# A hybrid decoder layer on one core: the first chunk's order around its constants, attention, second norm and first expert head

## The reference

```python
hn = modulate(rmsnorm(x, g_norm1), sh1, sc1)
xr, gr, q, k, v, gate_r, gate_a = split(hn @ w_in)
xc = causal_conv(xr);  hseq = rglru(xc)            # gates r, i; linear scan over time
y_r = (hseq * gelu(gr)) @ w_rnn_out
y_a = attention(rope(q), rope(k), v, window 128, sinks) @ w_attn_out   # 16 heads, 4 key heads
merged = sigmoid(gate_r) * y_r + sigmoid(gate_a) * y_a
x1 = x + gt1 * (merged @ w_out)
h2 = modulate(rmsnorm(x1, g_norm2), sh2, sc2)
# expert mixer: 8 heads, two sets of 128 keys per head, top 16 of each, top 16 of their sums
s = (h2 @ w_pq) . sub_keys;  e, g = top16 of pairs, softmax
out[t] = sum over the 128 chosen experts of g * gelu(h2[t] . u_tab[e]) * v_tab[e]
y = rmsnorm(x1 + gt2 * out, g_final)
```

## Time and profile before

| | us |
|---|---|
| median of 3 runs | 2088.82 |
| the three runs | 2089.44, 2076.90, 2088.82 |
| profiled execution | 2075.17 |
| its span in the profile | 2073.4 |
| busy in the span: PE / DVE / POOL / ACT | 1382.4 / 1238.5 / 1131.1 / 514.2 |
| gathers of `u_tab` and `v_tab` | 520 + 520, 545.33 MB of 701.78 MB |

### The profile page before, as it was taken

One profiled execution on the slowest core, in us unless ns is written; L12 is line 12 of the kernel. 1 busy time (PEld: TensorE's weight loads), 2 busy tenths in 40 slices (PEclk: granted clock), 3 DMA queues, 4 the chain that ended last, 5 costly groups with the idle time before them and its releaser, 6 DMA issues.

```text
span 2073.4 us, 22570 instructions
## 1 busy us (share of the span) xinstructions
PE 1382.4 (67%) x7058; PEld 882.5 (43%) x7058; DVE 1238.5 (60%) x3120; ACT 514.2 (25%) x1466; POOL 1131.1 (55%) x1046
## 2 busy tenths in 40 slices
PE   5998999877877677988877876433444444543444
PEld 5877888766654444666555643111111110111111
DVE  3255211376888788766658656656667656655640
ACT  2436200222345244112213322112111112211110
POOL 0000000046664466757756767777777777777774
PEclk9999999988998898979888987555555666656556
DMA  9745345499999799999999999999999999999997
GB/s 349 263 155 201 118 139 172 139 343 400 369 407 344 272 342 341 408 393 376 408 407 403 374 409 388 391 369 376 377 385 366 397 386 386 373 385 379 374 396 281
DMA packets 202294, 701.78 MB, mean 338 GB/s; under 512 B 22552, under 2 KB 32096, under 8 KB 201888
## 3 DMA queue, kind: packets, MB, share of 16 engines
q0 software_dynamic: 149760, 545.33, 68.2%
q1 hardware_dynamic: 52416, 155.02, 20.7%
HBM read 691.26 MB, written 11.06 MB: 339 GB/s over the span
## 4 chain that ended last, share of the span: by engine, by line
PE 26%; DVE 19%; DMA 18%; issue 17%; POOL 17%; ACT 3%; SPq 1%; POOLq 0%; DVEq 0%; ACTq 0%
POOL arena L1894 17%; PE acc L738 15%; DMA arena<-in_v_tab,pku 9%; DVE arena L1741 6%; DMA arena<-in_u_tab,pku 5%; PE y L1030 5%; DMA arena<-key_rows 3%; PE acc L777 2%; DVE pku L1762 1%; DMA arena<-w_mod 1%; DVE pk L1761 1%; PE acc L751 1%; DVE arena L1468 1%; DVE pku L1774 1%; DVE arena L1514 1%
## 5 line engine op out<-in xcount | busy, mean ns | idle before, releaser
L1894 POOL DMA_INDIRECT arena<-in_u_tab,pku x520 | 566.4, 1089 | 599.8 <-DVE pku L1800 336.5
L1741 DVE CUSTOM_DVE_ANT_0 arena<-arena 128x1024 f32<-128x1024 f32 x520 | 625.8, 1223 | 388.1 <-DMA arena<-in_u_tab,pku 379.1
L1894 POOL DMA_INDIRECT arena<-in_v_tab,pku x520 | 561.7, 1080 | 241.9 <-issue 145.4
L1030 PE MATMUL y<-arena 128*32 128x512 f32 x2080 | 417.0, 919 | 411.2 <-DMA arena<-in_v_tab,pku 410.5
L738 PE MATMUL acc<-arena 128*128 128x256 f32 (+1 forms) x2816 | 658.9, 394 | 33.5 <-DVE arena L1421 13.1
L738 PEld LDWEIGHTS acc<-arena 128*128 128x128 f32 x2816 | 545.6, 196 | 159.9 <-issue 64.4
L1030 PEld LDWEIGHTS y<-arena 128*32 128x32 f32 x2080 | 81.8, 144 | 645.2 <-issue 625.2
L1013 PE MATMUL turned<-arena 128*128 128x256 f32 x128 | 60.0, 561 | 135.9 <-DVE arena L1817 133.1
L1013 PEld LDWEIGHTS turned<-arena 128*128 128x128 f32 x128 | 26.7, 252 | 202.6 <-DVE arena L1817 195.3
L1301 ACT ACTIVATE pk<-pk 128x1 f32<-128x1 f32 x520 | 103.6, 281 | 2.1
L1298 ACT ACTIVATE pk<-pk 128x8 f32<-128x8 f32 x65 | 13.5, 208 | 301.6 <-DVE pk L1741 278.3
(11 more groups left out here) (210 smaller groups left out, 1354.4 us busy)
## 6 DMA issues: line engine op xcount, KB each, us to landing
arena<-w_mod SPq DMA_DIRECT2D x48, 512.0 KB, 5.8
arena<-w_pq SPq DMA_DIRECT2D x32, 512.0 KB, 6.7
arena<-w_xr SPq DMA_DIRECT2D x20, 512.0 KB, 9.3
arena<-w_qk SPq DMA_DIRECT2D x20, 512.0 KB, 6.9
arena<-w_gr SPq DMA_DIRECT2D x20, 512.0 KB, 6.7
arena<-w_rnn SPq DMA_DIRECT2D x16, 640.0 KB, 4.0
arena<-in_u_tab,pku POOLq DMA_INDIRECT x520, 7.7
arena<-in_v_tab,pku POOLq DMA_INDIRECT x520, 6.8
```

Of the source, the lines that this page charges most:

```text
L1030: mm = pe.matmul(y[rows, h, :], spread[g % NTURN][:, 32 * j:32 * j + 32], rows_v[j][:, h * 512:(h + 1) * 512], start=first and (g != SAMPL ...
L1741: dve.tensor_tensor_reduce(u_row[j], u_row[j], h_of[o], 1.0, 0.0, ALU.mult, ALU.add, dots[g % 2][:, j:j + 1]).then_inc(s_urd, 1)
L1894: pool.indirect_dma_start(out=row, out_offset=None, in_=table, in_offset=bass.IndirectOffsetOnAxis(ap=idx, axis=0), **more).then_inc(signa ...
```

## The change

It moves work in the order of all engines, and adds little:

- **Constants.** The identity and ones stay where they were. The attention mask, the smaller constants and the convolution state are loaded after `mod` piece 15 and no longer ahead of pieces 4 to 15; cos and sin after them too. They get a semaphore of their own, for which `turned_rows` waits.
- **Rotations.** The second batch of five scans is cut into 2, 2 and 1, with the rotations of query blocks 2 and 3 between.
- **Gate blocks.** `gr` 0 goes in front of the first scores and `gr` 1 behind them, in both chunks, and each step has one `gr`.
- **Second norm, chunk 0.** The sum of squares goes into the bank `turned`, one matmul behind each `out` block and the last by itself; ACT loads the root's table before the `out` blocks. The k-th matmul of `pq` 0 waits for the k-th row block of `h2T` alone.
- **First scores.** A product `first` behind `pq` 1 gives the scores of head 0; `PEER_FROM` is behind it, so `pq` 2 and on belong to the second stretch. Places for pieces are dealt accordingly.
- **Later heads.** `load_stage` is issued two quarters earlier (but for heads 1 and 16); head 1 is ranked two quarters later.
- **End.** DVE scales the last tile's sums straight from the bank `y`; ACT copies nothing, and loads the root's table ahead.

```diff
+GR_EARLY = 2
+GR_AT = ((2,), (3,), (4,), (5,), (6,), (7,), (8,), (9,))
-GR_AT = ((0,), (1,), (2, 3), (4,), (5,), (6, 7), (8,), (9,))
...
         mods(ch, "scores")
+        block(ch, "gr", 0)
         product(ch, "s", 0, (), 0.9)
         product(ch, "s", 1, (), 0.9)
+        block(ch, "gr", 1)
...
                 block(ch, "pq", c)
+                if ch == 0 and c == 1:
+                    product(0, "first", 0, (("keys", 0),), 0.5)
-PEER_FROM = NO[0, "keys", 0] + 1
+PEER_FROM = NO[0, "first", 0] + 1
-RANK_FROM = [PARTS * g - 2 * PARTS for g in FIRST_GROUP]
+RANK_FROM = [PARTS * g - 2 * PARTS + 2 * int(h == 1) for h, g in enumerate(FIRST_GROUP)]
+STAGE_AT = [f + 1 if h in (1, CT * PH) else f - 1 for h, f in enumerate(RANK_FROM)]
...
-                sp.dma_start(const[:, b:b + 4 * P], X["const"][:, a:a + 4 * P]).then_inc(s_const, 16)
+                sp.dma_start(const[:, b:b + 2 * P], X["const"][:, a:a + 2 * P]).then_inc(s_const, 16)
+                load_until((0, "mod", 15))
+                a, b = CONST_COLS["mask"][0], LOCAL_COLS["mask"][0]
+                sp.dma_start(const[:, b:b + 2 * P], X["const"][:, a:a + 2 * P]).then_inc(s_const2, 16)
                 a, b, w = CONST_COLS["iota"][0], LOCAL_COLS["iota"][0], TOPK + NKV + 3 * P
-                sp.dma_start(const[:, b:b + w], X["const"][:, a:a + w]).then_inc(s_const, 16)
+                sp.dma_start(const[:, b:b + w], X["const"][:, a:a + w]).then_inc(s_const2, 16)
                 sp.dma_start(states[:, RC * 3:RC * 27], X["conv_state"]).then_inc(s_conv0, 16)
-                load_until((0, "mod", 7))
...
-                if k - 1 in RANK_FROM[1:]:
-                    load_stage(RANK_FROM.index(k - 1, 1))
+                if k in STAGE_AT[1:]:
+                    load_stage(STAGE_AT.index(k, 1))
...
+                    if name == "pq" and c == 0:
+                        pe.wait_ge(s_h, 2 * DC * ch + DC + k + 1)
                     mm = pe.matmul(a[:, 0:n], w[:, k, :], rhs[:, k, 0:n], start=(k == 0), stop=(k == ks - 1))
...
+            def sum_early(k):
+                pe.wait_ge(s_sq, DC + k + 1)
+                return pe.matmul(turned[:, 0:CP], ones, squares2[:, k, 0:CP], start=(k == 0), stop=(k == DC - 1), skip_group_check=True)
...
+            def first_scores():
+                wk = await_piece(pe, (0, "keys", 0))[:, 0:4 * P].rearrange("p (c k) -> p c k", c=4)
+                yield NO[0, "first", 0]
+                a = take(0, "first", 0)
+                for c in range(2):
+                    await_read(pe, 0, "pq", c)
+                    mm = pe.matmul(a[:, c * P:(c + 1) * P], pq[0][:, c, 0:P], wk[:, c, :], start=True, stop=True)
+                mm.then_inc(s_ready, 1)
...
                     project(ch, "out", c, mg)
+                    if ch == 0 and c:
+                        sum_early(c - 1)
...
+                if ch == 0:
+                    yield NO[ch, "out", 0]
+                    act.activation(fstat[:, 3:4], eps, ACT.Sqrt)
...
-                scans(ch, 1)
+                scans(ch, 1, (5, 6))
+                yield NO[ch, "turn", QK_THEN[0]]
+                rotate(ch, QK_THEN[0])
+                scans(ch, 1, (7, 8))
+                yield NO[ch, "turn", QK_THEN[1]]
+                rotate(ch, QK_THEN[1])
+                scans(ch, 1, (9,))
+                scanned(ch, 1)
...
+                if o == TILES:
+                    act.activation(fstat[:, 3:4], eps, ACT.Sqrt)
+                    return
...
+                else:
+                    dve.wait_ge(s_store, 16 * tile)
+                    dve.wait_ge(s_vrd, 2 * (LAST_GROUP[o] + 1))
+                    link(dve.tensor_tensor(dst.rearrange("p (h n) -> p h n", h=2), y[:, :, :], gain.rearrange("p (h n) -> p h n", h=2), ALU.mult))
```

More of the change, by code:

```diff
@@ L214, in _slots @@
         late = int(FIRST[p] >= PEER_FROM)
+        if p == (0, "keys", 0):
+            place[1] = place[0] % (OWN + EXTRA) + 1
         s = place[late] % (OWN if late else OWN + EXTRA)
@@ L916, in chunk @@
                 yield from modulations(ch, "scores")
+                yield NO[ch, "gr", 0]
+                project(ch, "gr", 0, hT)
                 yield NO[ch, "s", 0]
                 yield from att_scores(ch, 0)
+                yield NO[ch, "gr", 1]
+                project(ch, "gr", 1, hT)
                 for i in range(STEPS):
@@ L954, in chunk @@
                     project(ch, "out", c, mg)
+                    if ch == 0 and c:
+                        sum_early(c - 1)
                 yield NO[ch, "norm", 1]
-                pe.wait_ge(s_sq, ch * 2 * DC + 2 * DC)
-                square_sum(ch, 1, squares2)
+                if ch == 0:
+                    take(0, "norm", 1)
+                    sum_early(DC - 1).then_inc(s_ready, 1)
+                else:
+                    pe.wait_ge(s_sq, ch * 2 * DC + 2 * DC)
+                    square_sum(ch, 1, squares2)
                 yield from modulations(ch, "norm")
@@ L966, in chunk @@
                         project(ch, "pq", c, h2T)
+                        if ch == 0 and c == 1:
+                            yield from first_scores()
                     yield NO[ch, "keys", (CT + ch) * pair]
@@ L1010, in turn @@
                     pe.wait_ge(s_mask, 1)
+                    await_read(pe, 0, "norm", 1)
                 else:
@@ L1076, in root @@
                 a = take(ch, "norm", which)
+                if ch == 0 and which:
+                    a = turned
                 release(act.activation((rstd, rstd2)[which][:, 0:n], a[:, 0:n], ACT.Sqrt, bias=eps, scale=1.0 / D), ch, "norm", which)
@@ L1238, in chunk @@
                         release(act.copy(pq[c // PH][:, c % PH, 0:n], a[:, 0:n]), ch, "pq", c)
+                        if ch == 0 and c == 1:
+                            yield NO[0, "first", 0]
+                            a = take(0, "first", 0)
+                            release(act.copy(stage[0], a[:, 0:2 * NKEYS]), 0, "first", 0)
                     for t in range(CT + ch):
@@ L1241, in chunk @@
                         yield NO[ch, "keys", m]
-                        if ch == 0 and m == 0:
-                            a = take(ch, "keys", 0)
-                            act.copy(stage[0], a[:, 0:2 * NKEYS]).then_inc(s_first, 1)
                         spill_rows(ch, "keys", m, rows_of(t))
@@ L1459, in variances, with scans @@
                     link(dve.tensor_tensor(gate_i[:, i, 0:n], gate_i[:, i, 0:n], xc[:, j, 0:n], ALU.mult))
-            def scans(ch, b):
+            def scans(ch, b, js):
                 n = TOK[ch]
-                for j in range(HALF5 * b, HALF5 * b + HALF5):
+                for j in js:
                     i = j % HALF5
@@ L1633, in chunk @@
                 yield NO[ch, "qk", 9]
-                scans(ch, 0)
+                scans(ch, 0, range(HALF5))
+                scanned(ch, 0)
                 for c in QK_FIRST[:-1]:
@@ L1648, in chunk @@
                     dve.sem_inc(s_state, 1)
-                for c in QK_THEN[:-1]:
+                for c in QK_THEN[2:-1]:
                     yield NO[ch, "turn", c]
@@ L1664, in chunk @@
                         att_normalise(ch, i + 1)
+                    if i == 0:
+                        for c in range(GR_EARLY):
+                            gate_rows(ch, c)
                     for c in GR_AT[i]:
@@ L1753, in best_keys @@
                 if head == 0:
-                    dve.wait_ge(s_first, 1)
+                    await_read(dve, 0, "first", 0)
                 else:
@@ L1836, in add_residual @@
                 dst, x, gain = (ysum, xin, gt2p) if tile < TILES else (hcur[1], xin_s, gt2s)
-                dve.wait_ge(s_yfree, o + 1)
-                link(dve.tensor_tensor(dst[0:rows, :], dst[0:rows, :], gain[0:rows, :], ALU.mult))
+                if o < TILES:
+                    dve.wait_ge(s_yfree, o + 1)
+                    link(dve.tensor_tensor(dst[0:rows, :], dst[0:rows, :], gain[0:rows, :], ALU.mult))
+                else:
+                    dve.wait_ge(s_store, 16 * tile)
+                    dve.wait_ge(s_vrd, 2 * (LAST_GROUP[o] + 1))
+                    link(dve.tensor_tensor(dst.rearrange("p (h n) -> p h n", h=2), y[:, :, :], gain.rearrange("p (h n) -> p h n", h=2), ALU.mult))
                 if tile < TILES:
```

14 lines of the change are left out of this document (9 added, 5 removed).

## The result

| | before | after |
|---|---|---|
| median of six runs, us | 2080.16 | 2057.47 |
| lowest and highest | 2075.58, 2089.44 | 2053.24, 2066.78 |
| profiled execution, its span | 2075.17, 2073.4 | 2057.22, 2055.0 |

The ratio is 0.9889, with an interval of 0.9851 to 0.9927: 1.1% faster, 15 to 31 us. The forecast of 2062.5 and its range of 2045 to 2080 hold the median; the profiled execution gained 18.0 us where the sum said 26.3. By medians the gain is thus 22.7 us here and 26.9 there. The two traces, on which the account by stretches rests, show less of it.

A forecast was written before the change was run, and what follows sets the result against it. PE bounds the stretch before the first gather, DMA transfers the rest. Front 20.0, chunk 1's first scores 4 and end 2.3 sum to 26.3 us off 2088.82: 2062.5 us, range 2045 to 2080.

The forecast's parts named there:

- Transfers bound the rest: From the first gather on: DMA engines are full, so an earlier first ranking, by 20.0 us, comes off the end.
- Constants: Before `mod` 3: 0.72 MB of constants and states no longer load ahead of its pieces, 1.8 us.
- norm and `pq` 0: Chunk 0's second norm and first query block: one sum hidden (0.5 us), per-row wait removes 2.20; together 2.7 us.
- end: After the last sums: ACT's copy (1.01 us) falls away and the root's table load (1.28) moves earlier, 2.3 us.
- Gate blocks: Chunk 0 attention: `gr` 1 fills PE's wait before the first transposes, two-block steps lose one each; 3.5 us.
- First scores: From `pq` 0 to the first ranking: two of four blocks stay ahead of it, 7.0 us earlier.
- What moves behind the first gather: Two `pq` blocks and a `keys` product, 8 us of PE: covered by PE's wait and DMA work, taken at 0.
- Chunk 1's first scores: There `gr` 1 fills PE's 6.55 us wait and POOL's 13.54 us wait shrinks: 4 us of DMA time.
- key rows: DVE's 28.5 us of waits for scores loaded back from HBM: mostly removed, but counted 0, bounds 0 to 8.
- The interleaved stretch sets its own pace: Rival, chance 0.2: DVE's order sets the interleaved stretch, moved PE work lengthens it; gain 14 us, 2074.5.
- More comes back: Rival, chance 0.12: key-row waits and most of chunk 1's hole were DMA time, 8 + 6 us more; 2048.
- Slower: Rival, chance 0.05: chunk 1's mixer sums lie behind blocks, POOL waits 13.54 us at four more steps; 2121.

The follow-up runs named there:

- late dealing: The changed kernel's sharing of `LIMITS` cost from `PEER_FROM`, so later products fall into later quarters; the like shift alone on the kernel before: ratio 0.9985.
- late loads: Changed kernel with stored scores loaded back at the old place, one quarter behind each `RANK_FROM`, for all heads: ratio 0.9922.
- best kernel: Changed kernel with the old kernel's dealing, chunk 0's places for query pieces 2 to 7, row stores first, chunk 1's gate block 1 gelu earlier: ratio 0.9802, median 2046.45.
- more PE work: Changed kernel with 18 unread matmuls (7.8 us of PE) added behind the first scores, ahead of query block 2: ratio 0.9878.
- same dealing: Changed kernel with cost shared out over the quarters from behind the first product with the keys, as before the change: ratio 0.9831, median 2050.96.

## Why the prediction was right, and where it was off

*Transfers bound the rest.* Right. In all traces the stretch from first gather to last sum, less the time lost, is 1588 to 1599 us. What the order alone can win there is in the 39 to 66 us lost. That the earlier front comes off the end one to one is what the two traces show (17.4 us at the first gather, 1.7 lost behind it, 2.3 at the end: 18.0), and it is not shown beyond them: the early first scores move the first gather by 6 to 8 us, and the ratios cannot tell that from nothing.

*Constants* 2.6 us (1.8), *rotations* 5.1 (5.0), *norm and `pq` 0* 2.5 (2.7; 0.4 of it the norm), *end* 2.3 (2.3): the mechanisms held, and the sizes within 0.8. By an estimate from the figure of the Trainium skill (ScalarE: Activation LUTs, "What ACT_TABLE_LOAD costs": 2.66 us a switch, and the copy's 1.01) the end would have gained 3.7; the trace's 2.3 does not bear that out.

*Gate blocks* 1.2 instead of 3.5: `gr` 1 filled the wait, but step 0 lasted 9.7 us where it was 9.34, and not the 8.3 that follow from taking 1.0 off. The prediction named ACT's extra gelu as the lower bound, and it took most. The rest is step 2, which lost its second block and still lasts 7.4 us (176.29 to 183.68, with a wait of 1.37 for DVE) and not 6.6. Doing this gelu earlier on ACT lost more in step 1 than it gave in step 0.

*First scores* 6.0 instead of 7.0: an overlooked part of the change, since the loads of query pieces 2 to 5 stand ahead of the four stores of rows in SP's order. With the stores first (8.54 us, was 16.31) it would be 7.8.

*What moves behind the first gather*, taken at 0 because PE's wait covers it. That is the step that failed. As work it is covered, though not as the prediction said: the two blocks and the product are done before the first gather, during the first ranking. But it also lengthens the list which `LIMITS` deals out, so that most later products meet other pieces of the mixer, and with the late dealing the changed kernel is 8 to 10 us slower. A further 2.0 us (0.77 MB at 388 GB/s) came from loads that I had said stay ahead of the first gather.

*Chunk 1's first scores* at 4: 0 to 4, and *key rows* at 0: some 8 us with an uncertainty of as much. "In none of these waits but around the hole" did the share fall: the hole was the place, and one wait of 5.99 us there goes with half of what the late loads lose. On these figures the two about cancel the dealing and the loads; in the two traces the stretch behind the first gather kept its length, and the sum lost the 4 that it had counted there. By medians it kept them: 22.7 to 26.9 us less the 17.4 of the front and the 2.3 of the end leave 3 to 7. Which of these holds is open.

*The number.* That 2062.5 came within 5 us of 2057.47 is in part luck. A term that the prediction did not have (the dealing) and one that it took at nothing (the key rows) are about as large and of opposite sign, and the median from which the sum was taken off, 2088.82 of three runs, became 2080.16 with six.

*The rivals.* "The interleaved stretch sets its own pace" gave 14 us and the right place, the interleaved stretch, but the wrong cause: not PE's work, which cost nothing when it was added once more; DVE's load by itself was not tested. "More comes back" asked for 40 us, which only the best kernel has. "Slower" by sums behind blocks did not come; POOL's longest waits for sums behind the first gather are one of 14.81, one of 9.28 and one of 8.64.

## What to carry to other kernels

Where a list of work is dealt out by cost over the steps of a loop, a change that adds to the list moves what stands behind it: look at what step each later product falls into, not only at the work that moved, and test the dealing by itself. When transfers bound a stretch, add up the time in which they stand still: that number is the most that any reordering can win, and it tells a wait under which the transfers stopped from one under which they went on. It is no measure of the time by itself: here 11 us more of it cost nothing in one kernel. A wait that is filled at one engine shows up at the next thing which that engine needs, here a bank that ACT had not read.

## What I had not expected of the hardware

The transfers between first gather and last sum took 1588.0 us in one execution (more PE work) and 1598.4 in another (same dealing), with 621.97 and 621.94 MB: 0.7% without a difference in bytes, as much as most of the effects here. A store of 256 KB that SP issued behind four loads of 512 KB held up ACT for 6.52 to 8.18 us in seven executions of that order, and for 1.57 and 1.11 us in the two kernels that issue it ahead of these loads.
